# Forty instead of 32 dense tokens as gathered rows in an expert layer's key stage, and twelve dots moved into its value stage

## The reference, cut to what matters

```python
def peer_ffn(h, w_q, sub_keys, u_tab, v_tab):          # 256 tokens, 8 heads, 128 x 128 experts, 16 picks a head
    q = (xc @ w_q).reshape(t, PEER_HEADS, 2, PEER_QDIM // 2)
    sc = jnp.einsum('thpc,hpnc->thpn', q, sub_keys)
    v_half, i_half = lax.top_k(sc, PEER_TOPK_HALF)
    ...                                                # top 16 of 16 x 16 sums: top_s, expert
    g = jax.nn.softmax(top_s, axis=-1)
    u = u_tab[expert]                                  # 128 rows of 1024 a token
    act = jax.nn.gelu(jnp.einsum('thkd,td->thk', u, xc), approximate=False)
    return jnp.einsum('thk,thkd->td', g * act, v_tab[expert])
```

## Time and profile before

| | us |
|---|---|
| median of three runs | 1942.85 (1938.29 to 1945.58) |
| the profiled execution | 1940.13 |
| its span | 1938.4 |
| TensorE busy | 1887.6 (97%) |
| VectorE busy | 1594.6 (82%) |
| ScalarE busy | 970.4 (50%) |
| GpSimd busy | 413.2 (21%) |
| moved by DMA | 546.57 MB, mean 282 GB/s |
| granted TensorE clock, mean | 0.997 |

### The profile page before, as it was taken

The page is one execution under the profiler, slowest core; times in us unless marked ns, Lnnn a source line. Parts: engine busy times, 40 slices in busy tenths (PEclk is TensorE's granted clock), DMA queues, the critical chain, the costliest instruction groups (busy, mean ns, idle before and its releaser), DMA issues.

```text
span 1938.4 us, 33523 instructions
## 1 busy us (share of the span) xinstructions
PE 1887.6 (97%) x11716; PEld 1683.7 (87%) x11716; DVE 1594.6 (82%) x3038; ACT 970.4 (50%) x1898; POOL 413.2 (21%) x348
## 2 busy tenths in 40 slices
PE   8999999999999999999999999999999999999998
PEld 7888887878999999987788888899999998877776
DVE  6899886886898879688888977779978886888887
ACT  6557644565311545355565666541135444555555
POOL 0000000000233344332232100003335442322220
PEclk9999999999999999999999999999999999999999
DMA  6544334525599999999999853359999999999995
GB/s 259 224 177 179 136 99 144 177 78 179 204 408 409 398 364 392 399 315 334 333 354 341 295 184 114 103 182 360 408 398 384 363 403 342 336 325 329 339 327 184
DMA packets 140841, 546.57 MB, mean 282 GB/s; under 512 B 14620, under 2 KB 14748, under 8 KB 138048
## 3 DMA queue, kind: packets, MB, share of 16 engines
q1 hardware_dynamic: 93760, 376.33, 54.2%
q0 software_dynamic: 46976, 168.91, 22.7%
HBM read 543.02 MB, written 1.05 MB: 281 GB/s over the span
## 4 chain that ended last, share of the span: by engine, by line
PE 57%; DMA 14%; DVE 10%; ACT 3%; issue 3%; SPq 0%; ACTq 0%; DVEq 0%
PE bank L2654 24%; DMA wbuf<-in_peer_v 10%; PE bank L350 7%; PE bank L352 7%; PE bank L351 7%; DMA wbuf<-in_peer_u 5%; PE bank L2685 3%; PE bank L2686 3%; PE bank L2503 2%; DVE tile_lo L3082 2%; ACT tile_hi L2807 1%; DVE x_tok L2440 1%; DVE tile_lo L280 1%; PE bank L2611 1%; DVE w_parts L3086 1%
## 5 line engine op out<-in xcount | busy, mean ns | idle before, releaser
L2654 PE MATMUL bank<-h_dense,wbuf 128*128 128x160 f32 x4096 | 575.0, 300 | 7.0 <-DMA wbuf<-in_peer_u 6.7
L2654 PEld LDWEIGHTS bank<-h_dense,wbuf 128*128 128x128 f32 x4096 | 558.7, 190 | 12.0 <-issue 6.9
L2807 ACT ACTIVATE tile_hi<-wbuf 128x1024 fp32r<-128x1024 f32 x248 | 261.5, 1056 | 243.8 <-DMA wbuf<-in_peer_v 211.2
L3082 DVE TENSOR_TENSOR tile_lo<-wbuf,tile_hi 128x1024 fp32r<-128x1024 f32 x256 | 308.4, 1221 | 77.5 <-ACT tile_hi L2807 75.6
L2416 POOL DMA_INDIRECT e_gbuf<-in_peer_v,e_row_at x128 | 174.1, 1360 | 405.6 <-DVE x_tok L2440 370.8
L2685 PE MATMUL bank<-tile_hi,w_parts 128*128 128x512 f32 x512 | 203.9, 398 | 8.8 <-DVE tile_lo L3082 5.6
L2416 POOL DMA_INDIRECT e_gbuf<-in_peer_rows,e_row_at x128 | 157.7, 1232 | 250.9 <-DVE e_dots L2434 138.5
L2686 PE MATMUL bank<-tile_lo,w_parts 128*128 128x512 f32 x512 | 199.8, 390 | 0.0
L352 PE MATMUL bank<-tile_hi,w_parts 128*128 128x512 f32 x512 | 199.4, 389 | 0.0
L350 PE MATMUL bank<-tile_hi,w_parts 128*128 128x512 f32 x512 | 199.4, 389 | 0.0
L351 PE MATMUL bank<-tile_lo,w_parts 128*128 128x512 f32 x512 | 199.4, 389 | 0.0
(11 more groups left out here) (426 smaller groups left out, 3614.9 us busy)
## 6 DMA issues: line engine op xcount, KB each, us to landing
wbuf<-in_peer_u SPq DMA_DIRECT2D x128, 1024.0 KB, 9.9
wbuf<-in_peer_v SPq DMA_DIRECT2D x256, 512.0 KB, 6.3
wbuf<-in_w_in SPq DMA_DIRECT2D x16, 2048.0 KB, 7.3
wbuf<-in_peer_q SPq DMA_DIRECT2D x32, 512.0 KB, 4.1
wbuf<-in_hyb_in SPq DMA_DIRECT2D x16, 512.0 KB, 4.0
wbuf<-in_mla_uq SPq DMA_DIRECT2D x9, 512.0 KB, 3.7
wbuf<-in_mla_in SPq DMA_DIRECT2D x8, 528.0 KB, 4.7
wbuf<-in_w_v SPq DMA_DIRECT2D x2, 2048.0 KB, 7.2
```

The source lines that it names most:

```text
L2654: last = nc.tensor.matmul(bank[:, j // 2 % 2, j % 2 * S + EXTRA:j % 2 * S + DENSE], deep[:, slot, k * P:(k + 1) * P], h_dense[:, k, PLAIN] ...
L2807: nc.scalar.activation(tile_hi[:, slot, 0:D], ring[:, slot, 0:D], ACT.Copy).then_inc(hi_done, 1)
L3082: nc.vector.tensor_tensor(tile_lo[:, slot, 0:D], ring[:, slot, 0:D], tile_hi[:, slot, 0:D].bitcast(F32), ALU.subtract).then_inc(lo_done, 1)
```

## The change

The gathered part of the dense tokens grows from 32 to 40, as a second block (32, 8): tokens 32 to 39, with 128 / 8 = 16 slots of 8 picks. So SPREAD is 40, DOTS 104, ITEMS 168; the product with U has 152 columns; 19 plain groups and 10 FEW groups instead of 20 and 8; each of the three kinds of moves has 4 + 16 DMAs instead of 4. The second block's row numbers are moved ahead of gather 48, its dots ahead of gather 64, once item 56 is done.

Of the 104 dots, 92 (FIRST_ITEMS) are taken in the key stage, the other twelve are the first items of the value stage. `x_gathered` moves out of w_parts' way and `x_few` (two pieces) takes the region; ScalarE's wait for all dots becomes one for the 56 that use x_few. The gelus of the gathered tokens' dots move from pair 58 and value tile 1 to value tiles 4 and 27. The schedule's numbers move with it.

```diff
-BLOCKS = ((0, 32),)
+BLOCKS = ((0, 32), (32, 8))
...
-            "x_gathered": nc.alloc_sbuf_tensor_at("x_gathered", [P, D], F32, offset=h_at + LINE * 4 + KT * DENSE * 4 + SLOTS * 2 * DENSE * 4),
+            "x_few_at": h_at + LINE * 4 + KT * DENSE * 4,
...
-    KEYS_TURNED = 50
-    FEW_TURNED_BEHIND = 11
-    WEIGHTS_AT = [53 + 5 * n // 2 + 2 * (n > FEW_TURNED_BEHIND) for n in range(PLAIN_GROUPS)]
+    KEYS_TURNED = 46
+    FEW_TURNED_BEHIND = 14
+    WEIGHTS_AT = [49 + 5 * n // 2 + 2 * (n > FEW_TURNED_BEHIND) for n in range(PLAIN_GROUPS)]
...
-    x_few = [sb(f"{tag}_x_few{n}", [P, D]) for n in range(len(BLOCKS))]
+    x_gathered = sb(f"{tag}_x_gathered", [P, D])
+    x_few = [nc.alloc_sbuf_tensor_at(f"{tag}_x_few{n}", [P, D], F32, offset=g["x_few_at"] + 4 * D * n) for n in range(len(BLOCKS))]
...
     def taken_at(tile):
 
-        return min(34 + (tile - 48) * (DOTS - 34) // (121 - 48), DOTS + max(0, tile - 121) // 2)
-
-    TAKEN, LAST_TAKE = (30, 33, 35), 123
-    EXPS_AT, FEW_AT = (11, 23), 35
-    ACTS_AT, ACTS = 58, (slice(0, 48), slice(48, SHARED))
-    FEW_MULTIPLIED, FEW_KEPT = 8, 13
+        return min(32 + (tile - 44) * (FIRST_ITEMS - 32) // (125 - 44), FIRST_ITEMS)
+
+    TAKEN, LAST_TAKE = (27, 30, 32), 123
+    EXPS_AT, FEW_AT = (11, 21), 38
+    FIRST_ITEMS = DOTS - 12
+    ACTS_AT, ACTS = (4, 27), (slice(0, 48), slice(48, SHARED))
+    ACTS_ROUNDS = ACTS_AT[-1] // STEP + 1
+    FEW_MULTIPLIED, FEW_KEPT = 12, 13
...
-            if f == ACTS_AT:
-                acts_of(ACTS[0])
...
-                if a:
-                    act.wait_ge(gather_used, GATHER_0 + DOTS)
+                if a == 0:
+                    act.wait_ge(gather_used, GATHER_0 + EARLY + SPREAD)
...
-        for j in range(STEP):
-            value_tile(0, j)
-            if j == 1:
-                acts_of(ACTS[1])
-        with act.Fori(1, ROUNDS - 1) as r:
+        for tile in range(ACTS_ROUNDS * STEP):
+            value_tile(tile // STEP, tile % STEP)
+            if tile in ACTS_AT:
+                acts_of(ACTS[ACTS_AT.index(tile)])
+        with act.Fori(ACTS_ROUNDS, ROUNDS - 1) as r:
```

More of the change, by code:

```diff
@@ L2284, in expert_layer @@
     ring, tile_hi, tile_lo = g["ring"], g["tile_hi"], g["tile_lo"]
-    h_dense, w_parts, x_gathered = g["h_dense"], g["w_parts"], g["x_gathered"]
+    h_dense, w_parts = g["h_dense"], g["w_parts"]
     lo_done, hi_done, used = g["lo_done"], g["hi_done"], g["used"]
```

## The result

The changed kernel takes 1962.8 us in the median (1956.4 to 1966.9), the kernel before beside it 1940.6: a ratio of 1.0135, 95% interval 1.0114 to 1.0157. It is slower by 1.35%; forecast were 1961 us. The profiled execution took 1966.94 us, its span 1965.2.

A forecast was written before the change was run, and what follows sets the result against it. It took TensorE, hardly ever idle, and the value stage's V-tile load loop to be at their limits together. Per layer -12.2 + 0.5 - 1.0 + 14.0 + 9.1 = +10.4 us; 1940.1 + 20.8 = 1961 us, range 1941 to 1990.

The forecast's parts named there:

- (e): Key stage, pair 38: ScalarE waits for sixteen small moves, stalling TensorE 12.3 us, plus 1.7 of clock: 14.0 us a layer.
- (a): Both expert stages: eight columns fewer in each of 2048 matmuls save 6.3 ns each, 12.9 us a layer.
- (b): Key stage up to tile 50: loads set the pace, so 4.4 us gained instead of 5.1; with (a) 12.2.
- (c): Key stage, one-hot weights: 19 plain and 10 small groups instead of 20 and 8 cost 0.5 us a layer.
- R5: Rival: loads set the pace further along the key stage, columns bring about 5 us, 1977; chance 0.16 together with R4.
- (d): Key stage, stall behind the turning of gathered activations: one multiply fewer ahead gains 1.0 us of 1.37.
- (f): Value stage: more gathers delay V tiles; by period = (landing + 2.9) / 4 this costs 9.1 us a layer.
- R2: Rival: key-stage stall doesn't come, as POOL issues or lands faster, but value-stage cost does: 1933 us; chance 0.10.
- R1: Rival: the value stage absorbs its gathers, the key-stage stall remains: 1943 us; chance 0.15.
- R3: Rival: neither the key-stage stall nor the value-stage cost comes: 1915 us; chance 0.07.
- R4: Rival: the value-stage loop costs its upper bound, and the stall comes too: 1989 us; chance 0.16 together with R5.

The follow-up runs named there:

- experiment 2: Changed kernel with ScalarE's wait for the sixteen moves at pair 42 instead of 38, VectorE's product two groups later: 1931.4 us, ratio 0.9965; again 1933.1, 0.9978.
- experiment 8: experiment 2 with eight gathered rows fewer dotted before the turn of the picks, made up for later: 1945.5 us, ratio 1.0050.
- experiment 5: experiment 2 with all 104 dots kept in the key stage, none moved to the value stage: 1934.6 us, ratio 0.9980.
- experiment 6: experiment 2 with six dots moved to the value stage instead of twelve: 1928.7 us, ratio 0.9966.
- experiment 4: Kernel before (32 gathered tokens, its key-stage places) with the last twelve dots in the value stage: 1947.6 us, ratio 1.0052.
- Experiment 7: Three kernels: experiment 2 with value-stage dots over 8 columns, 1930.6 us; kernel before with fourteen more VectorE passes, 1945.9; with fourteen more gathers, 1950.3.
- experiment 3: Changed kernel with ScalarE's wait for the sixteen moves at pair 40 instead of 38, the product behind group 13: 1949.7 us, ratio 1.0071.

## Why the prediction came out

The sum was right to 2 us, and the largest term by its mechanism. That the rest came so near is in part luck: three terms were off and partly cancelled.

- **(e), the new wait: right.** The chain was put at 16.5 us from the gelu to the landing; it was 15.7 (706.65 to 722.32). The idle time was 11.1 and 10.8 us for 12.3, the clock's part 0.8 + 1.3 = 2.1 us in layer one for 1.7 (the group 1.86 for 1.08, 48 matmuls 7.70 for 6.41). The whole step came to 13.9 us (experiment 2) for 14.0, a wait put 1.2 to 1.5 us too long and a clock price put 0.4 to 1.2 too low. The sixteen issues took 8.23 us, 0.514 each, for 0.52. The moves landed after 3.8 to 6.1 us, in the median 4.9. The 5.3 us of the sum had been read from moves of 4 KB; these are of 0.2 KB. So the 2.0 us fixed time that the Trainium skill gives (DMA: Bandwidth & Descriptors, Anatomy of one DMA) would again have been too short here, and by far in experiment 8 (11.2). The second sixteen moves cost nothing, as predicted: POOL waited 6.18 us behind them, TensorE not at all.
- **(a) and (b), the columns: (a) right, (b) too good by some 2 us, with a wrong working.** Key stages without the stall are 302.0 us in the mean, for 312.4 before: 10.4 less. The prediction's terms but (e) give 12.7. TensorE's busy time in layer one fell by 12.3 us in experiment 2 (294.93 for 307.20), where (a) and (c) give 12.4. What failed is the working of (b). It credited four tiles at 2.44 us each and three rows at 3.8 us. But 2.44 us at 409 GB/s are a tile of U and nine tenths of a gather already: the gathers were counted twice. Seven loads of 0.524 MB, four tiles and three gathers, are 9.0 us; the turn came 10.3 us earlier (116.5 us into the stage before, 106.2 after), not 12.8.

```profile
626.81 2.33 PE L2657 MATMUL bank<-h_dense,wbuf 128*128 128x152 f32 x16 [0.56 <-DMA wbuf<-in_peer_u]
628.99 0.27 PE L2599 MATMUL bank<-cst,e_stage 128*128 128x128 f32 x1
```

- **What (a) did not say.** How much the columns pay hangs on the gathers left in the key stage: 16.0 us for both layers at the 98 items of before, 20.9 at the 92 of the change, and 4.8 when 104 stay (experiments 5 and 6). The prediction held the loads (R5) to be no limit behind tile 50. At 92 and 98 items that was nearly right; at 104 they are one.
- **(d): mis-sized.** The stall behind the turning of the activations went from 1.37 to 1.02 us, 0.35 gained for 1.0.

```profile
758.11 1.08 PE L2504 MATMUL bank<-e_hot_shares,e_hot_keys 128*128 128x128 f16 x16 [1.02 <-ACT e_hot_shares L2485]
```

- **(f), the value stage: mis-sized, and the mechanism not as told.** Forecast were 9.1 us a layer, measured 7.6, and 5.6 in the executions without a stall in the key stage. The step rested on V tiles that land later, 6.8 us. They don't, going by the median: 6.4 and 6.6 for 6.3 and 6.6. From these landings (landing + 2.9) / 4 gives 2.33 and 2.38 us a tile; the stages took 2.38 and 2.42. What grew is ScalarE's wait for them in layer one (116.8 for 95.0 us) and TensorE's for VectorE's rest of the hidden weights (12.8 us over both layers, 3.1 before, while its waits for tile_lo fell from 5.6 to 0.8). Form of the first row as in the earlier trace rows, the second the page's group:

```profile
L2808 ACT ACTIVATE tile_hi<-wbuf 128x1024 fp32r<-128x1024 f32 x124 | 131.4, 1059 | 124.3 <-DMA wbuf<-in_peer_v 116.8 <-PE bank L352 7.2
L2688 PE MATMUL bank<-tile_hi,w_parts 128*128 128x512 f32 x512 | 207.0, 404 | 14.5 <-DVE w_parts L3087 12.8
```

  ScalarE's wait can't be the price by itself: in experiment 4 it is 233.4 us over both layers (before 211.2, changed 234.8), beside value stages of 599.9. Experiment 7 shows that added gathers are enough to lengthen the stage. Through which tiles they act, with the median landing unchanged, stays open, and so does why passes alone cost nearly as much.
- **Not in the sum at all:** 4.3 us ahead of the first key stage, in unchanged code. Across the kernels here its start lay between 516.4 and 524.3 us; within one kernel it repeated within 1.0 us (518.1 and 519.1, 522.8 and 523.0, twice 517.9). Yet the same matmul of an earlier layer (line 1336) starts at 404.27 and 406.81 us in the two executions of the kernel before, and at 407.34 and 407.55 in those of the changed one. So part of the 4.3 can be what two executions of one kernel differ by; what sets it stays open.
- **The rivals.** R2 (no stall) is what experiment 2 built: 1933 forecast, 1931 and 1933 measured. R1 (the value stage takes its gathers for nothing) and R3 fall with the value stages' 15.3 us, R4 because they are far from the 40 that it asks. R5 fits only the 104 items of experiment 5.

## What to carry to other kernels

When a wait is moved or its work grows, write down what has to happen between its trigger and its landing, and place the wait behind that by the program's own order: here four pairs were worth 28 us. Leave room for a slow landing, which was 11 us once where 5 had been usual. Where two limits lie within a few per cent of each other, price one part of a change with the other held where it was, and at more than one value: narrower matmuls were worth 20.9, 16.0 or 4.8 us with 92, 98 or 104 items beside them. And in a stretch that loads limit, a period already holds everything that was loaded in it; count its bytes once.

## What was not expected of the hardware

- The clock fell for short gaps too, and its price is paid behind the gap: after 11.08 us idle 0.8 us on the group and 1.3 on the next 48 matmuls, after 10.78 us (layer two) 0.8 and 2.1 (8.49 us for 6.41). After 4.64 us (experiment 3) the group took 1.87 us as well, with the same 0.50 over five us:

```profile
721.00:725.00 4.00, 0.01 (x1) 0.00 (x0) 1.80 (x3) 2.50 (x9) 0.00 (x0) 0.91 1.02 416
725.00:730.00 5.00, 4.36 (x27) 4.39 (x28) 4.41 (x8) 3.32 (x12) 3.81 (x2) 0.50 0.22 52
```

- After 2.92 us idle (experiment 5) the group took 1.86 us, with 0.50 over the next five. After 2.82 us (experiment 3, layer two) and 1.75 us (experiment 8) it took its 1.08.
- The queues' busy share was 0.99 to 1.01 at 382 to 397 GB/s over whole key stages, and 1.03 at 409 over 80 us; in the value stages 0.95 stood beside only 347. VectorE began to wait for gathered rows between the key stages of experiment 6 (1.00, 393 and 394 GB/s, no such wait) and of experiment 5 (1.00 and 1.01, 393 and 397; 5.3 and 6.9 us): neither number told the two apart.
- The landing of sixteen moves of 0.2 KB had its median at 4.9 us in the changed kernel and at 11.2 in experiment 8.
- Two executions of one kernel, 4 us apart in all, differed by 7.7 us in a single value stage, and by 2.3 the other way in the other one.
